# Transposing the experts' gated rows: four PE transposes and a PSUM copy against one transposing DMA per step

## The reference

```
x = LayerNorm(alpha * x + gate1 * (concat(A, B, C) @ w_out[l]))
x = LayerNorm(alpha * x + gate2 * FFN_l(x * (1 + scale2) + shift2))
FFN: SwiGLU (even l) / top-2-of-8 SwiGLU experts (odd l)
expert e:  y = (silu(h @ w1[e]) * (h @ w3[e])) @ w2[e],   w1, w3: 1024 x 1024,   w2: 1024 x 1024
```

## Time and profile before

| | us |
|---|---|
| median of three runs | 2339.85 |
| profiled execution, its own time | 2339.42 |
| its span | 2337.6 |
| TensorE matmul busy | 2101.0 (90%) |
| VectorE busy | 1437.2 (61%) |
| ScalarE busy | 1266.3 (54%) |
| GpSimd busy | 751.5 (32%) |
| mean busy share of the DMA engines in slices 31 to 36 of 40 | 0.7 to 0.9 |

### The profile page before, as it was taken

How to read it: one execution, slowest core, us unless ns; L and a number is a source line. 1 busy time by engine, 2 the same in 40 slices (tenths; PEclk the granted TensorE clock), 3 DMA queues, 4 the chain that set the end, 5 groups by cost and what they waited for, 6 DMA issues and landing times.

```text
span 2337.6 us, 53990 instructions
## 1 busy us (share of the span) xinstructions
PE 2101.0 (90%) x22874; PEld 1285.3 (55%) x22874; DVE 1437.2 (61%) x1779; ACT 1266.3 (54%) x1651; POOL 751.5 (32%) x546
## 2 busy tenths in 40 slices
PE   4999787978989999999899879878879999999994
PEld 3666456845565555555667557645544444444441
DVE  3362656668362121215558667585379999999975
ACT  3534554556444242424543765465378777777762
POOL 0332115433404242424223236432123333333332
PEclk9999898989999999999999989989979999999997
DMA  9442690020312222224231000100367788991124
GB/s 290 138 145 94 217 289 30 4 59 4 93 37 92 71 90 72 86 75 143 90 119 39 1 11 4 45 18 23 131 230 226 240 272 280 321 344 54 32 91 166
DMA packets 246503, 278.45 MB, mean 119 GB/s; under 512 B 61345, under 2 KB 221965, under 8 KB 246159
## 3 DMA queue, kind: packets, MB, share of 16 engines
q1 hardware_dynamic: 237056, 251.99, 34.4%
q0 software_dynamic: 6128, 21.50, 2.5%
q10 hardware_dynamic: 3103, 1.85, 0.3%
HBM read 359.97 MB, written 29.11 MB: 166 GB/s over the span
## 4 chain that ended last, share of the span: by engine, by line
PE 75%; DVE 9%; ACT 8%; issue 3%; DMA 2%; POOL 1%; SPq 1%; DVEq 0%; ACTq 0%; POOLq 0%
PE ps L2307 74%; DVE arena L1674 1%; ACT mix L1460 1%; DVE arena L1678 1%; DVE mix L1674 1%; DMA wbuf<-in_w_mod 1%; DVE small L1902 1%; SPq L726 1%; PE ps L3074 1%; ACT arena L1170 1%; DVE hT L1674 1%; ACT hT L1466 1%; POOL extra L915 1%; ACT arena L1051 1%; DVE const L1674 1%
## 5 line engine op out<-in xcount | busy, mean ns | idle before, releaser
L2307 PE MATMUL ps<-hT,mix 128*128 128x512 f16 (+2 forms) x3024 | 378.1, 287 | 22.7 <-DVE hT L1674 10.4
L2307 PE MATMUL ps<-w,xgT 128*128 128x512 f16 x1632 | 365.6, 381 | 3.6 <-ACT xgT L1571 3.6
L2307 PEld LDWEIGHTS ps<-hT,mix 128*128 128x128 f16 x3024 | 227.4, 99 | 171.1 <-issue 20.7
L2220 DVE SCALAR_TENSOR_TENSOR w<-wst,w 128x2048 f16<-128x2048 f32 x136 | 312.2, 2334 | 5.9 <-ACT w L1557 5.9
L1035 POOL TENSOR_TENSOR a<-aval,a 128x256 f16<-128x256 f32 x68 | 163.3, 2401 | 366.2 <-ACT a L1593 366.2
L2307 PEld LDWEIGHTS ps<-w,xgT 128*128 128x128 f16 x1632 | 157.4, 98 | 182.5 <-ACT xgT L1571 3.9
L1557 ACT ACTIVATE w<-wst 128x2048 f16<-128x2048 f32 x136 | 251.6, 1899 | 3.1 <-DMA xs_rows<-htok,slot_i 3.0
L2307 PE MATMUL ps<-mix 128*128 128x512 f16 (+5 forms) x1856 | 203.3, 287 | 6.2 <-ACT mix L1251 5.7
L2307 PE MATMUL ps<-hT,arena 128*128 128x128 f16 (+1 forms) x1440 | 199.4, 299 | 0.0
L2307 PE MATMUL ps<-w2m,aT 128*128 128x512 f16 x816 | 190.6, 384 | 5.5 <-DVE aT L2247 5.5
L2226 DVE SCALAR_TENSOR_TENSOR w2m<-wst,w2m 128x2048 f16<-128x2048 f32 x68 | 156.0, 2294 | 26.0 <-ACT w2m L1565 25.5
(11 more groups left out here) (354 smaller groups left out, 3464.5 us busy)
## 6 DMA issues: line engine op xcount, KB each, us to landing
wst<-in_moe_w SPq DMA_DIRECT2D x204, 1024.0 KB
wbuf<-in_w_mod SPq DMA_DIRECT2D x40, 1024.0 KB
wbuf<-in_ffn_w SPq DMA_DIRECT2D x33, 1024.0 KB
wbuf<-in_w_in SPq DMA_DIRECT2D x20, 1024.0 KB
xs_rows<-in_table SPq DMA_DIRECT2D x17, 512.0 KB, 6.3
ys_rows<-yb POOLq DMA_DIRECT2D x17, 512.0 KB, 3.2
wbuf<-in_w_out SPq DMA_DIRECT2D x32, 256.0 KB
mix<-in_w_mod SPq DMA_DIRECT2D x1, 4096.0 KB
```

What stands on the lines that cost most here:

```text
L2220: v_.scalar_tensor_tensor(out=q[1], in0=staged(s, p), scalar=WS, in1=q[0], op0=ALU.mult, op1=ALU.subtract).then_inc(sg["m_lo13"], 1)
L2307: return mm_(o, w, x, start=first, stop=last, skip_group_check=True)
```

## The change

TensorE's four transposes and VectorE's copy of step s go. In their place SP issues one transposing DMA from `a16` (128 rows of 512 float16) to `aT`, on the queue of the weights, in its iteration s+2 behind the w2 fetch. It waits for the low half (`m_alo`), and from s = 3 on for `down(s-3)`, which read the same of the three `aT` buffers. `a16` gets four buffers in place of two; the split w2 gets a third. TensorE's order becomes `up(s)`, `down(s-3)`. A tile is summed in banks 6 and 7 or in banks 2 and 3 in turn, and written out one step later. The five `rowg` fetches and the `xr` fetches now stand behind the last transposing DMA in SP's list.

```diff
+            def turned(s):
+                sp.wait_ge(sg["m_alo"], s + 1)
+                if s >= 3:
+                    sp.wait_ge(sg["m_down"], s - 2)
+                sp.dma_start_transpose(aT[:, s % 3, :].rearrange("p (c n) -> p c n", n=P),
+                                       a16[s % 4][:, :, :].rearrange("p i n -> p (i n)")).then_inc(at_in[s % 3], 16)
...
-            for s in range(MS):
+            for s in range(MS + 2):
...
                 if 4 <= s + 1 < MS:
                     sp.wait_ge(sg["m_lo2"], s - 2)
                     stage(bass.ds(owner[(s + 1) // MQ], 1), s + 1, 2, fresh[(s + 1) // MQ])
+                if 0 <= s - 2:
+                    turned(s - 2)
...
-                if s >= 2:
-                    act.wait_ge(sg["m_down"], s - 1)
+                if s >= 3:
+                    act.wait_ge(sg["m_down"], s - 2)
...
-                    if s >= 2:
-                        act.wait_ge(sg["m_turn"], s - 1)
-                    a.activation(a16[:, s % 2, 0, :], aval[:, s % 2, :], ACT.Copy).then_inc(sg["m_ahi"], 1)
+                    if s >= 4:
+                        act.wait_ge(at_in[(s - 4) % 3], 16 * ((s - 4) // 3 + 1))
+                    a.activation(a16[s % 4][:, 0, :], aval[:, s % 2, :], ACT.Copy).then_inc(sg["m_ahi"], 1)
...
-                if 0 <= s - 2 < MS:
-                    dve.wait_ge(sg["m_turn"], s - 1)
-                    if s - 2 >= 3:
-                        dve.wait_ge(sg["m_down"], s - 4)
-                    v_.tensor_copy(aT[:, (s - 2) % 3, :], bank[2 + s % 2].bitcast(F16)[:, 0:512]).then_inc(sg["m_at"], 1)
...
             def down(s):
                 j, q = divmod(s, MQ)
-                pe.wait_ge(sg["m_at"], s + 1)
+                pe.wait_ge(at_in[s % 3], 16 * (s // 3 + 1))
                 pe.wait_ge(sg["m_lo2"], s + 1)
-                if q == 0 and j:
-                    pe.wait_ge(sg["m_yact"], j)
-                    pe.wait_ge(sg["m_ydve"], j)
+                if q == 0 and j >= 2:
+                    pe.wait_ge(sg["m_yact"], j - 1)
+                    pe.wait_ge(sg["m_ydve"], j - 1)
...
-            for s in range(MS + 2):
+            for s in range(MS + 3):
                 if s < MS:
                     up(s)
-                if 0 <= s - 2:
-                    down(s - 2)
-                if 0 <= s - 1 < MS:
-                    turn_a(s - 1)
+                if 0 <= s - 3:
+                    down(s - 3)
```

More of the change, by code:

```diff
@@ L358, in backbone_kernel @@
                enumerate((ADDR["xT"], ADDR["xT"] + 16384, ADDR["wbuf"]))]
-        w2m = [over(f"w2m_{i}", [P, 2048], a) for i, a in enumerate((ADDR["xT"] + 32768, ADDR["wbuf"] + 16384))]
+        HG = ADDR["const"] + 4 * CONST_AT["hg"][0]
+        w2m = [over(f"w2m_{i}", [P, 2048], a) for i, a in enumerate((ADDR["xT"] + 32768, ADDR["wbuf"] + 16384, HG))]
         htok = over("htok", [P, TT, D], ADDR["wbuf"])
-        HG = ADDR["const"] + 4 * CONST_AT["hg"][0]
         x1tok = over("x1tok", [P, 4, D], HG)
@@ L367, in backbone_kernel @@
         aval = over("aval", [P, 2, 256], ADDR["va"] + 3072)
-        a16 = over("a16", [P, 2, 2, 256], ADDR["lbt"], F16)
+        a16 = [over(f"a16_{i}", [P, 2, 256], a, F16) for i, a in
+               enumerate((ADDR["lbt"], ADDR["lbt"] + 1024, ADDR["states"], ADDR["states"] + 1024))]
         id16 = over("id16", [P, P], ADDR["revb"], F16)
@@ L524, in backbone_kernel @@
             "hot_ready m_hot g2_out zero_in id_ready x1_first x1_out picked_ready slots_ready tiles_ready gates_ready xs_out "
-            "m_hi13 m_lo13 m_hi2 m_lo2 m_xt m_xhi m_xlo m_up m_silu m_act m_ahi m_alo m_turn m_at "
+            "m_hi13 m_lo13 m_hi2 m_lo2 m_xt m_xhi m_xlo m_up m_silu m_act m_ahi m_alo "
             "m_down m_yact m_ydve row_in xr_in dg_ready y_psum y_mul lnv_ready lnr_ready lnb_ready").split()}
@@ L528, in backbone_kernel @@
         xg_in = [sem(f"xg_in{i}") for i in range(2)]
+        at_in = [sem(f"at_in{i}") for i in range(3)]
         yg_in = [sem(f"yg_in{i}") for i in range(TT)]
@@ L544, in backbone_kernel @@
         w13p = [[h.rearrange("p (k n) -> p k n", k=KT) for h in halves(w13[i][:, :], 4096, 4096)] for i in range(3)]
-        w2p = [[h.rearrange("p (t n) -> p t n", t=2) for h in halves(w2m[i][:, :], 2048, 2048)] for i in range(2)]
+        w2p = [[h.rearrange("p (t n) -> p t n", t=2) for h in halves(w2m[i][:, :], 2048, 2048)] for i in range(3)]
         bank = [ps[:, b // 2, (b % 2) * 512:(b % 2) * 512 + 512] for b in range(8)]
@@ L1026, in _ @@
                                             htok[:, t, :], None).then_inc(sg["xs_out"], 16)
-            for s in range(MS + 3):
-                if s >= 6 and s % MQ == 2:
-                    j = (s - 6) // MQ
+            for s in range(MS + 4):
+                if s >= 7 and s % MQ == 3:
+                    j = (s - 7) // MQ
                     pool.wait_ge(sg["m_yact"], j + 1)
@@ L1034, in _ @@
                     pool.wait_ge(sg["m_ahi"], s + 1)
-                    g.tensor_tensor(a16[:, s % 2, 1, :], aval[:, s % 2, :], a16[:, s % 2, 0, :],
+                    g.tensor_tensor(a16[s % 4][:, 1, :], aval[:, s % 2, :], a16[s % 4][:, 0, :],
                                     ALU.subtract).then_inc(sg["m_alo"], 1)
@@ L1560, in upper2 @@
                 act.wait_ge(st_full[3 * (s % MQ) + 2], staged_at(3 * (s % MQ) + 2, s // MQ + 1))
-                if s >= 2:
-                    act.wait_ge(sg["m_down"], s - 1)
+                if s >= 3:
+                    act.wait_ge(sg["m_down"], s - 2)
                 elif s == 1:
                     act.wait_ge(sg["xs_out"], 16 * 2 * TT)
-                a.activation(w2p[s % 2][0], staged(s, 2), ACT.Copy, scale=WS).then_inc(sg["m_hi2"], 1)
+                a.activation(w2p[s % 3][0], staged(s, 2), ACT.Copy, scale=WS).then_inc(sg["m_hi2"], 1)
             upper13(0)
@@ L1578, in _ @@
                         act.wait_ge(ys_out[j % 2], 16 * (j // 2))
-                    a.activation(yb[j % 2][:, 0:512], bank[6], ACT.Copy, scale=IWS).then_inc(sg["m_yact"], 1)
+                    a.activation(yb[j % 2][:, 0:512], bank[6 - 4 * (j % 2)], ACT.Copy, scale=IWS).then_inc(sg["m_yact"], 1)
                 if s + 2 < MS:
@@ L2224, in lower2 @@
                 dve.wait_ge(sg["m_hi2"], s + 1)
-                q = w2p[s % 2]
+                q = w2p[s % 3]
                 v_.scalar_tensor_tensor(out=q[1], in0=staged(s, 2), scalar=WS, in1=q[0], op0=ALU.mult,
@@ L2240, in _ @@
                         dve.wait_ge(ys_out[j % 2], 16 * (j // 2))
-                    v_.tensor_scalar(yb[j % 2][:, 512:1024], bank[7], IWS, None, ALU.mult,
+                    v_.tensor_scalar(yb[j % 2][:, 512:1024], bank[7 - 4 * (j % 2)], IWS, None, ALU.mult,
                                      ALU.bypass).then_inc(sg["m_ydve"], 1)
-                if 0 <= s - 2 < MS:
-                    dve.wait_ge(sg["m_turn"], s - 1)
-                    if s - 2 >= 3:
-                        dve.wait_ge(sg["m_down"], s - 4)
-                    v_.tensor_copy(aT[:, (s - 2) % 3, :], bank[2 + s % 2].bitcast(F16)[:, 0:512]).then_inc(sg["m_at"], 1)
                 if s + 2 < MS:
@@ L3087, in down @@
                         for h in range(2):
-                            ins = mm(bank[6 + h], x, w2p[s % 2][b_][:, t, h * 512:h * 512 + 512],
+                            ins = mm(bank[6 - 4 * (j % 2) + h], x, w2p[s % 3][b_][:, t, h * 512:h * 512 + 512],
                                      (q, t, a_ + b_) == (0, 0, 0), (q, t, a_) == (MQ - 1, 1, 1))
                 ins.then_inc(sg["m_down"], 1)
-            for s in range(MS + 2):
+            for s in range(MS + 3):
                 if s < MS:
                     up(s)
-                if 0 <= s - 2:
-                    down(s - 2)
-                if 0 <= s - 1 < MS:
-                    turn_a(s - 1)
+                if 0 <= s - 3:
+                    down(s - 3)
             pe.wait_ge(sg["m_act"], MS)
```

## The result

The changed kernel takes 2349.31 us (median of 20 runs, 2343.45 to 2354.08), the kernel before in the same sessions 2343.68 (20 runs, 2335.29 to 2351.06). The ratio is 1.0027 with a 95% interval of 1.0018 to 1.0037: 6.3 us slower, 4 to 9. The forecast was 12.6 us slower.

What follows compares the result with a forecast made beforehand. TensorE was taken to bound the loop, the DMA queue second in runs of new experts. 2339.4 - 23.3 (gains) + 28.7 (waits for turns) + 3.7 (clock) + 3.5 (behind the loop) = 2352.0 us; forecast 2352, range 2318 to 2378.

Steps and rivals of the forecast that it cites:

- The start: At `up(3)`: no longer behind `down(0)`, it needs only its weights and `aval` of step 1; 7.1 us earlier.
- The end: After `up(67)` begins: the last `down` ends 16.1 us later in place of 18.2; gain 2.1 us.
- the two runs: Consecutive new-expert tiles, 6 and 7 (two), 9 to 11 (three): TensorE waits 8p - 4.3 and 5.0 + 12p us there.
- p: Price of one turn (transposing DMA) on the weights' loaded queue: taken as 1.4 us, between 0.9 and 2.0.
- 20p + 0.7: TensorE's waits for turns in both runs of new experts together, at price p each: 28.7 us.
- The clock: TensorE at the end of each run of new experts: slow matmuls after idling, 1.85 us each, 3.7 us lost.
- Behind the loop: Late `rowg` and `xr` fetches meet the last store and gathers: 3.5 us lost, bounds nothing and 8 us.
- A: Rival: turns land in time, only 3.5 us behind the loop against 23.3 gained; 2320 us; chance 0.22 (p below 0.5).
- B: Rival: turns cheap, gap small, p from 0.5 to 1.0; 11 to 21 us of waiting, 2334 to 2346; chance 0.26.
- the forecast's case: Turns in the runs of new experts cost p from 1.1 to 2.4; 2347 to 2375 us; chance 0.46.
- C: Rival: each turn costs a whole `rows_of`, p = 3.7; 2415 us; chance 0.06 with what lies between.
- D: Rival: nothing moves on the chain, VectorE or ScalarE taking over TensorE's pace; 2339 us; chance next to nothing.

## Why the prediction was right, and where its sizes were off

- The bound and the gains: right. The period fell from 7.99 to 7.77 as read from the chain; 14.1 us forecast, 14.3 measured. The start: 7.1 forecast; 8.1 between the two profiles, and 7.1 between the two kernels without fetches (24.8 and 17.7 us from `up(0)` to `up(3)`). The end: 2.1 forecast, 2.5 measured. Sum 23.3 against 24.9. Of the 2.5, some 1.7 is the clock of one execution: without fetches the kernel before has the same wait of 2.12 us at its end, its clock doesn't fall, and the gain is 0.9.
- The place of the loss: right, and shown by taking the weights away. The waits stand at turns that lie among the weights of the two runs, and nowhere else in the loop. The tiles are those of the turns, 5 and 6, 9 and 10, and not those of the weights, as the prediction's "tiles 9 to 11" and "6 and 7" have it; its due times for steps 25 and 41 were set at the right places. The waits sum to 5.2 us in the run of two, within the 3 to 12 named as a sign, and to 10.4 in the run of three, under its 15 to 30. The due time against the landing of `rows_of` was the right reading: the turn of step 40 landed 30.8 us after its low half, with 18.1 us of room.
- The loop's loss was mis-sized: 28.7 us of waits and 3.7 of slow clock forecast, 32.4 together, 22.7 measured. The term that failed is the price of a turn, p = 1.4, in the step "with a quarter of the bytes and a smaller gap": I carried most of the gap ahead of a loaded `rows_of` into each turn. With the clock's 3.6 us (next point) taken off, 20p + 0.7 gives 19.1 us at p = 0.92; the two runs by themselves give 1.2 and 0.7, and a second turn per step cost 0.54. So p lies under 1.4 by each reading, but no one price fits both runs. The extra turn's wait at `down(13)` also says that single tiles have less room than "about 10 us".
- The clock: right in size. At the end of each run one slow `down` adds 1.7 (`down(24)`) and 1.9 us (`down(40)`), 3.6 against 3.7. The third slow one, `down(37)`, was hidden, as "inside a run where TensorE waits anyway this is hidden" says. The kernel with `rowg` and `xr` early has the same loop. There the same wait left the clock alone, two later `down`s waited 1.14 and 1.15 us instead, and `up(3)` to `up(67)` took 520.3 us against 520.0:

```profile
2056.29 2.76 PE L2316 MATMUL ps<-w2m,aT 128*128 128x512 f16 x12 [3.81 <-DMA aT<-a]
...
2065.37 2.76 PE L2316 MATMUL ps<-w2m,aT 128*128 128x512 f16 x12 [1.14 <-DMA aT<-a]
...
2074.46 2.76 PE L2316 MATMUL ps<-w2m,aT 128*128 128x512 f16 x12 [1.15 <-DMA aT<-a]
```

So the split of the 22.7 us into idle time and slow clock differs between executions; their sum is what repeats.
- Behind the loop: 3.5 forecast with bounds of 0 and 8, 6.3 measured. The mechanism is shown: with `rowg` and `xr` early it is gone. I had priced half of the gathers; it was the store ahead of them, 8.8 us in place of 2.9, that met the traffic.
- Of the rivals, A (turns in time) fell. B's condition, p from 0.5 to 1.0, covers 0.54 and 0.92, the forecast's 1.1 to 2.4 neither. By its time the result lies in the forecast's case (2347 to 2375), by its mechanism in B's, whose 2334 to 2346 it misses by 3 us; the store behind the loop and a kernel before that came out 3.8 us longer carried it over. The forecast's difference was twice the measured one. The 6.3 us are less than the 7 us that the prediction took for the least a measurement can tell; 20 runs of each tell them. C and D fell.
- The absolute time: 2352 forecast, 2349.3 measured. That it is nearer than the difference is luck: the kernel before itself came out 3.8 us above the three runs shown.
- Slips in the recorded sums: by them p = 1.0 gives 2344 and not 2346, p = 2.4 gives 2372 and not 2375, and C 2408 and not 2415. What frees the issue at s = 42 is w2 of step 38, not 39; the time of 2057.8 stands.

Why some turns meet a gap and others don't stays open. Half-microsecond windows of the changed kernel ahead of the turn that TensorE waited for until 2094.8 show one (59 and 16 GB/s), and those ahead of the turn that landed at 2050.9 don't:

```profile
2049.00:2049.50 0.50, 0.50 (x4) 0.20 (x3) 0.50 (x1) 0.42 (x1) 0.00 (x0) 1.00 1.00 391
2049.50:2050.00 0.50, 0.50 (x5) 0.20 (x2) 0.50 (x2) 0.00 (x0) 0.00 (x0) 1.00 1.59 290
2050.00:2050.50 0.50, 0.36 (x2) 0.00 (x0) 0.50 (x1) 0.10 (x1) 0.00 (x0) 1.00 0.89 243
...
2092.50:2093.00 0.50, 0.00 (x0) 0.00 (x0) 0.50 (x1) 0.50 (x1) 0.50 (x1) 0.50 3.39 232
2093.00:2093.50 0.50, 0.00 (x0) 0.00 (x0) 0.50 (x2) 0.50 (x2) 0.50 (x1) 0.50 0.91 59
2093.50:2094.00 0.50, 0.00 (x0) 0.00 (x0) 0.50 (x1) 0.50 (x1) 0.42 (x1) 0.50 0.06 16
2094.00:2094.50 0.50, 0.00 (x0) 0.00 (x0) 0.50 (x1) 0.50 (x1) 0.00 (x0) 0.50 1.14 286
```

The Trainium skill (Advanced Engine Details and Errata, "X-Bar Transpose (TRN2)") has transposes as fast as plain DMAs. The rates here differ: in the kernel before a `rows_of` crosses at 290 GB/s with nothing else on the queue, where plain fetches reach 376:

```profile
2124.50:2125.75 1.25, 1.25 (x8) 0.54 (x7) 1.25 (x1) 0.68 (x2) 0.00 (x0) 1.00 1.28 290
```

What a turn costs a loaded queue beyond its bytes isn't settled: 0.54 us against 0.37 for the same bytes plain, one profile each.

## What to carry to other kernels

Before you put a step's hand-over on a queue, write down its room (when it is ready, when it is due) beside the latest landing on that queue under its worst load; a lateness that fetches four steps ahead bear unseen is a stall for a transfer with two steps of room. Read an engine's order apart from its work: three quarters of this change's gain at the ends was the later `down` alone, which with the transposes kept is 0.9975 (0.9961 to 0.9988) of before. Where both are wanted, buy room first: with `down(s-4)`, `rowg` early and `xr` last, turning by DMA comes to 0.9953 (0.9934 to 0.9971), faster than both kernels. Its interval overlaps that of the later `down` alone, so that turning by DMA beats TensorE's transposes in that order isn't shown.

## What the runs showed of the hardware

- Issuing a transposing DMA of 131,072 B takes 1.2 us of SP's or ScalarE's time on an empty queue, against 0.37 to 0.39 for a plain fetch of 1 MB (a fetch that the register condition skips takes 0.07 to 0.09). It lands after 2.4 us in the middle unloaded and after 7 to 12 us with the DMA engines full, on its own queue too (8.4 in the middle against 8.9).
- Beside a run of weights the issuing engine itself is held: 6 to 10.5 us for a `rows_of`, which takes 1.9 to 2.6 us to issue in the kernel before where no weights move. It was so on SP, where weights lie ahead on the queue, and on ScalarE, whose queue has none (up to 7.6 us).
- A stall doesn't always cost the clock. A wait of 3.8 us was followed by 12 matmuls of 5.30 us in the changed kernel and of 2.76 in the one with early `rowg` and `xr`; a wait of 2.12 us by 4.43 in the kernel before and by 2.76 in the same without fetches:

```profile
2285.39 2.76 PE L2307 MATMUL ps<-w2m,aT 128*128 128x512 f16 x12 [2.12 <-DVE aT L2247]
```
